# Norms of a latent attention placed between its projections, and products of split fp32 operands joined in pairs

## The reference

```python
# layer 0's mixer: sliding-window heads beside latent (MLA) heads
qa, ka, va, cq, ckv, kr = jnp.split(h @ w_in, EVEN_SPLITS, axis=-1)
qb = (rms_norm(cq, q_norm) @ w_uq)         # 384 -> 8 heads x (64 + 32 rotary)
kvb = (rms_norm(ckv, kv_norm) @ w_ukv)     # 256 -> 8 heads x (64 key + 64 value)
q_rope, k_rope = rope(q_rope, positions), rope(kr[:, :, None, :], positions)   # kr is shared by the heads
o = concat([window_attention(rope(qa), rope(ka), va), latent_attention(...)]) @ w_out
# gated network of the first block
x = x + (silu(h @ w_gate) * (h @ w_up)) @ w_down            # 1024 -> 2816 -> 1024
# second block: merge of three branches, then the last network
h = h + g1 * ((gp * (pool_o @ w_po) + gs * (sgu_o @ w_so) + ga * (attn_o @ w_ao)) @ w_o)
h = h + g2 * (square(relu(modulate(rms_norm_2(h)) @ w1)) @ w2)   # 1024 -> 4096 -> 1024
```

## Time and profile before

| | |
|---|---|
| median of 3 runs | 2077.81 us |
| profiled execution | 2079.3 us, its span 2077.5 us, mean granted clock 0.981 |
| busy | TensorE 97%, its weight loads 86%, VectorE 55%, ScalarE 43%, GpSimd 8% |
| matmuls | 14,920 |
| HBM read | 306.54 MB, 152 GB/s over the span |
| chain that ended last | TensorE 89%, VectorE 5%, ScalarE 2%, DMA 2% |

### The profile page before, as it was taken

The page is one execution under the profiler, slowest core; times in us unless marked ns, Lnnn a source line. Parts: engine busy times, 40 slices in busy tenths (PEclk is TensorE's granted clock), DMA queues, the critical chain, the costliest instruction groups (busy, mean ns, idle before and its releaser), DMA issues.

```text
span 2077.5 us, 35508 instructions
## 1 busy us (share of the span) xinstructions
PE 2007.5 (97%) x14920; PEld 1790.2 (86%) x14920; DVE 1139.2 (55%) x1987; ACT 888.3 (43%) x1498; POOL 165.5 (8%) x187
## 2 busy tenths in 40 slices
PE   7799999999999999999999999999999999999998
PEld 6759899999789999878688877777777987999998
DVE  6565565667556656524434445444444645666665
ACT  5464543444655445424532334322222435455443
POOL 0030000001203100002510000000000003000000
PEclk9899999999999999989999999999999999999999
DMA  7264589965647575313533324455454431664554
GB/s 222 66 194 155 152 221 218 228 183 161 226 143 190 177 216 170 107 41 121 160 101 98 107 84 142 157 162 174 158 166 143 127 92 30 184 196 146 183 183 132
DMA packets 331613, 317.71 MB, mean 153 GB/s; under 512 B 17061, under 2 KB 315820, under 8 KB 331198
## 3 DMA queue, kind: packets, MB, share of 16 engines
q1 hardware_dynamic: 326580, 301.64, 47.7%
q0 software_dynamic: 3904, 12.03, 3.0%
q10 hardware_dynamic: 970, 1.76, 0.3%
HBM read 306.54 MB, written 8.85 MB: 152 GB/s over the span
## 4 chain that ended last, share of the span: by engine, by line
PE 89%; DVE 5%; ACT 2%; DMA 2%; issue 1%; POOL 0%; ACTq 0%; DVEq 0%; POOLq 0%
PE acc L673 25%; PE acc L674 24%; PE acc L675 24%; DVE w_low L1894 2%; PE pss L838 2%; PE acc L688 1%; PE acc L689 1%; PE acc L690 1%; PE pst L850 1%; PE acc L761 1%; DMA raw<-in_l_w_up 1%; PE acc L821 1%; PE acc L865 1%; PE pso L865 1%; PE acc L789 1%
## 5 line engine op out<-in xcount | busy, mean ns | idle before, releaser
L1894 DVE TENSOR_TENSOR w_low<-raw,w_high 128x1024 fp32r<-128x1024 f32 (+4 forms) x503 | 560.5, 1154 | 174.5 <-ACT w_high L1371 173.7
L1371 ACT ACTIVATE w_high<-raw 128x1024 fp32r<-128x1024 f32 (+4 forms) x503 | 471.5, 984 | 398.7 <-PE acc L675 359.9
L673 PE MATMUL acc<-normed,w_high 128*128 128x256 f32 (+2 forms) x2008 | 636.7, 317 | 3.5 <-DVE w_low L1894 3.3
L674 PE MATMUL acc<-normed,w_high 128*128 128x256 f32 (+2 forms) x2008 | 631.3, 314 | 0.0
L675 PE MATMUL acc<-normed,w_low 128*128 128x256 f32 (+2 forms) x2008 | 630.9, 314 | 0.0
L673 PEld LDWEIGHTS acc<-normed,w_high 128*128 128x128 f32 (+1 forms) x2008 | 384.9, 192 | 32.4 <-DVE w_low L1894 4.4
L675 PEld LDWEIGHTS acc<-normed,w_low 128*128 128x128 f32 (+1 forms) x2008 | 385.0, 192 | 22.7
L674 PEld LDWEIGHTS acc<-normed,w_high 128*128 128x128 f32 (+1 forms) x2008 | 385.2, 192 | 22.1
L673 PE MATMUL acc<-inner,w_high 128*128 128x256 f32 (+2 forms) x1264 | 394.6, 312 | 3.4 <-DVE inner L1907 2.4
L674 PE MATMUL acc<-inner,w_high 128*128 128x256 f32 (+2 forms) x1264 | 391.8, 310 | 0.0
L675 PE MATMUL acc<-inner,w_low 128*128 128x256 f32 (+2 forms) x1264 | 391.2, 310 | 0.0
(11 more groups left out here) (255 smaller groups left out, 2123.2 us busy)
## 6 DMA issues: line engine op xcount, KB each, us to landing
raw<-in_w_ff SPq DMA_DIRECT2D x128, 512.0 KB, 4.4
raw<-in_w_mod SPq DMA_DIRECT2D x96, 512.0 KB, 4.6
raw<-in_w_in SPq DMA_DIRECT2D x84, 512.0 KB, 4.1
raw<-in_l_w_gate SPq DMA_DIRECT2D x44, 512.0 KB, 5.7
raw<-in_l_w_up SPq DMA_DIRECT2D x44, 512.0 KB, 4.7
raw<-in_l_w_down SPq DMA_DIRECT2D x32, 512.0 KB, 4.6
raw<-in_l_w_qkv SPq DMA_DIRECT2D x24, 512.0 KB, 4.4
raw<-in_l_w_out SPq DMA_DIRECT2D x16, 512.0 KB, 4.5
```

The lines of the kernel that those rows point to most:

```text
L673: mm(dst, lh, rh, start=i == 0, stop=False)
L674: mm(dst, lh, rl, start=False, stop=False)
L1371: nc.scalar.activation(WH[:, s % NSPLIT, w0:w0 + nw], RAW[:, r:r + nw], ACT.Copy)\
L1894: V.tensor_tensor(WL[:, s % NSPLIT, c], RAW[:, r:r + nw], WH[:, s % NSPLIT, c].bitcast(F32), ALU.subtract).then_inc(w_low, 1)
```

## The change

1. The query's mean square follows cq directly; its spread lies between the two tiles of ckv's unit; the rotations follow; the key's mean square lies between the query heads 0 to 3 and 4 to 5, its spread before the last two heads. ScalarE squares the query and takes its root before Silu and the sines, and the key after ckv's copy; VectorE makes both last sets of angles earlier, and norms the query before the rotations and the key after them. The sines have a semaphore of their own (`sin_done`), for which GpSimd and VectorE wait.
2. The shared rotary key leaves the lead: its sine product (`key_turned`) and its addition into eight heads (`key_spread`) stand in turns 1 and 2 of attention, behind the maxima.
3. `side_by_side` takes the place of `project` for output products and for the last network in layer 1, where there are 256 tokens: w_high meets high and low in one matmul of 512 columns that fills a bank, w_low x high goes onto its first half. Each bank then holds one tile in two halves, which the reader adds: `residual_sums` for the residual, and in the last network's input units a copy on ScalarE, two additions and a joined relu-square on VectorE. Excepted are the first unit of each mixer's output, layer 1's middle output stage of the gated network, and all products over 512 tokens.

The core of the diff (other places only follow the new count of banks):

```diff
 kr = wk(1792, 1, S, p0=64, p1=96)
+kr_turned = wk(3328, 1, S, p0=64, p1=96)
 cq = wk(2048, 3, S)
 ckv = wk(2816, 2, S)
-sq_cq, sq_ckv = wk(3328, 3, S), wk(4096, 2, S)
+sq_cq, sq_ckv = wk(3328, 3, S), view(BIAS, 2048, (2, S))
 mv = wk(2048, NB, 512)
...
+    def both(high, low):
+        return bass.AP(tensor=high.tensor, offset=high.offset,
+                       ap=[list(high.ap[0]), [low.offset - high.offset, 2], [1, S]])
+    def side_by_side(n, src, kt=KD, ready=None):
+        for i in range(n):
+            wh, wl = grid(take(kt, 2 * P), kt, 2 * P)
+            tiles = ([bank(), bank()],) if ready is not None and i == 0 else ([None], [None])
+            for n_group, group in enumerate(tiles):
+                if group[0] is None:
+                    group[0] = bank()
+                for k in range(kt):
+                    if ready is not None and i == 0:
+                        need(ready(k))
+                    high = src.high[:, k, 0:S]
+                    two = both(high, src.low[:, k, 0:S])
+                    for j, b in enumerate(group):
+                        m = j + n_group
+                        c = slice(P * m, P * m + P)
+                        out = b[:].rearrange("p (a n) -> p a n", a=2)
+                        if k == 0:
+                            mm(out, wh[:, k, c], two, start=True, stop=False)
+                            mm(b[:, 0:S], wl[:, k, c], high, start=False, stop=False)
+                        else:
+                            mm(b[:, 0:S], wl[:, k, c], high, start=False, stop=False)
+                            ins = mm(out, wh[:, k, c], two, start=False, stop=k == kt - 1)
+                            if k == kt - 1:
+                                ins.then_inc(acc_full, 1)
+            used()
...
             if u == 3:
-                pe.wait_ge(res_done, 1)
-                if k == KD - 1:
-                    copied(g)
+                copied(g + k - (KD - 1))
...
             project(1, at_pair, m=1)
-            project(1, at_pair)
             mean_square(sq_cq, 3, S)
+            w, b = grid(take(KD, 256), KD, 256), bank()
+            for m in range(2):
+                c = slice(P * m, P * m + P)
+                ins = product(b[:, S * m:S * m + S],
+                              [((w[0][:, k, c], w[1][:, k, c]),
+                                (at_pair.high[:, k, 0:S], at_pair.low[:, k, 0:S])) for k in range(KD)])
+                if m == 0:
+                    spread(S)
+            ins.then_inc(acc_full, 1)
+            used()
+            pe.wait_ge(const_in, 32)
+            rotate(swa_raw, const("rot64"), "swa", st["acc"] - 3)
+            st["store"] += 2
+            need(st["store"])
+            w = grid(take(3, 576), 3, 576)
+            turned(w, [96 * h for h in range(4)], cqn, 3, S, M=96)
...
             mean_square(sq_ckv, 2, S)
-            spread(S)
-            pe.wait_ge(const_in, 32)
-            rotate(swa_raw, const("rot64"), "swa", st["acc"] - 1)
+            turned(w, [96 * h for h in range(4, 6)], cqn, 3, S, M=96)
+            used()
             spread(S, at=S)
-            st["store"] += 3
-            need(st["store"])
-            turned(grid(take(3, 576), 3, 576), [96 * h for h in range(6)], cqn, 3, S, M=96)
-            used()
             turned(grid(take(3, 192), 3, 192), [0, 96], cqn, 3, S, M=96)
             used()
             heads = lambda x, k: x[:, k, :].rearrange("p (h d) -> p h d", h=8)[:, :, 64:128]
             def mla_lead():
                 wh, wl = w = grid(take(2, 1024), 2, 1024)
+                need(st["store"])
                 turned(w, [P * h for h in range(8)], ckvn, 2, S)
                 rotate(mla_raw, const("rot_mla"), "mla", st["acc"] - 5)
                 for t in range(NB):
                              for k in range(2)]).then_inc(acc_full, 1)
                 used()
-            attention(swa_tasks + mla_tasks, MODS, lead=mla_lead, tail=heads_product, late=SWA_H // 2)
+            st["store"] += 1
+            attention(swa_tasks + mla_tasks, MODS, lead=mla_lead, tail=heads_product, late=SWA_H // 2,
+                      keys=st["acc"] - 3)
...
         pe.wait_ge(cols_free, st["pair"])
-        project(3, ot)
...
         base = st["store"]
         st["store"] += KD
-        project(4, merged(T), T, ready=lambda k: base + k + 1)
+        if l:
+            side_by_side(4, merged(T), ready=lambda k: base + k + 1)
+        else:
...
             if kind == "in":
                 for m in range(tiles // 2):
-                    project(1, at_pair, T, ready=ready)
+                    if l:
+                        side_by_side(1, at_pair, ready=ready)
+                    else:
...
                 for m in range(D // cols):
-                    project(1, hidden(c, T), T, m=cols // P, kt=tiles)
+                    if l:
+                        side_by_side(1, hidden(c, T), kt=tiles)
...
                     if last and m:
-                        turn_out(m - 1, st["acc"] - 2)
...
+    pool.wait_ge(sin_done, 1)
...
-            copy_out(ckv, shape2)
-            split()
+            st["res"] = [st["acc"] - 2, st["acc"] - 1]
+            squares(cq, sq_cq, 3, S, res=True)
+            root(3, S)
             c = vcol["c_2"]
             nc.scalar.activation(SILC[:, :, 0:2].rearrange("p k s -> p s k"),
                                  VEC[:, c:c + 16].rearrange("p (s k) -> p s k", s=2), ACT.Silu)
             act.wait_ge(angles, 1)
-            nc.scalar.activation(ROPE[:], ROPE[:], ACT.Sin)
-            act.drain().then_inc(chain["act"], 1)
-            act.wait_ge(chain["act"], 1)
-            squares(cq, sq_cq, 3, S)
-            squares(ckv, sq_ckv, 2, S)
-            root(3, S)
+            nc.scalar.activation(ROPE[:], ROPE[:], ACT.Sin).then_inc(sin_done, 1)
+            split()
+            highs(chunks(cqn, 3, S))
+            copy_out(ckv, shape2)
+            st["res"] = [st["acc"] - 1]
+            squares(ckv, sq_ckv, 2, S, res=True)
+            split()
+            st["acc"] += 3
+            for i in range(2):
+                copy_out(mq[0:96, 2 * i:2 * i + 2, :], lambda b: shape2(b)[0:96], 96 ** -0.5)
             root(2, S, at=S)
-            st["acc"] += 3
-            highs(chunks(cqn, 3, S) + chunks(ckvn, 2, S))
-            for i in range(3):
-                copy_out(mq[0:96, 2 * i:2 * i + 2, :], lambda b: shape2(b)[0:96], 96 ** -0.5)
+            copy_out(mq[0:96, 4:6, :], lambda b: shape2(b)[0:96], 96 ** -0.5)
+            highs(chunks(ckvn, 2, S))
             split()
             copy_out(mq[0:96, 6:8, :], lambda b: shape2(b)[0:96], 96 ** -0.5)
             split()
...
-                    for n in banks(2, T):
+                    if l:
+                        for j in range(2):
+                            b, free = bank()
+                            nc.scalar.activation(SM[:, st["sig"] % 2, S * j:S * j + S], b[:, S:2 * S],
+                                                 ACT.Copy).then_inc(relu_done, 1)
+                        st["sig"] += 1
+                        highs([hidden(c, T).tiles(m, m + 2)])
+                    for n in banks(2, T) if l == 0 else ():
                         b, free = bank()
                         g, i = st["acc"] - 1, st["sig"]
...
+    def key_turned():
+        b, free = bank()
+        V.tensor_tensor(kr_turned[:, 0, :], b[64:96, 0:S], sin_mla(kr)[:, 0, :], ALU.mult).then_inc(free, 1)
+        st["rot"] += 1
+        own(free)
+    def key_spread():
+        rep = lambda a: bass.AP(tensor=a.tensor, offset=a.offset, ap=[list(a.ap[0]), [0, MLA_H], [1, S]])
+        dve.wait_ge(rot_done, st["rot"])
+        turned(V.tensor_tensor(mk[64:96, :, :], rep(kr), rep(kr_turned[:, 0, :]), ALU.add))
+    def rope(raw, sinv):
         dve.wait_ge(stored, st["store"])
         for i, r in enumerate(raw):
             b, free = bank()
...
-                rep = lambda a: bass.AP(tensor=a.tensor, offset=a.offset,
-                                        ap=[list(a.ap[0]), [0, MLA_H], [1, S]])
-                turned(V.tensor_tensor(wide, rep(r), rep(tmp), ALU.add))
-            else:
-                turned(V.tensor_tensor(r, r, tmp, ALU.add))
+            turned(V.tensor_tensor(r, r, tmp, ALU.add))
...
+        for k in m:
+            b, free = bank()
+            x = XC[:, k, 0:S]
+            for j in range(2):
+                half = b[:, S * j:S * j + S]
+                if gate is None:
+                    ins = V.tensor_tensor(x, x, half, ALU.add)
+                else:
+                    ins = V.scalar_tensor_tensor(x, half, MODC[:, gate + k, 0:1], x, ALU.mult, ALU.add)
+                if j == 0:
+                    link(ins)
+            ins.then_inc(free, 1)
+            own(free)
...
                 inverse(2 * j - 1)
+            if j <= len(between):
+                between[j - 1]()
...
             split()
             memory(0, 0, 2)
+            angle(2)
+            angle(3)
             split()
```

(46 more changed lines are left out.)

81 lines of the change are left out of this document (53 added, 28 removed).

## The result

The changed kernel takes 2057.8 us by the median (2054.95 to 2059.37, 4 runs) beside 2078.73 for the kernel before (2075.93 to 2083.92, 4 runs): a ratio of 0.9896 (95% interval 0.988 to 0.9913). The forecast was 2054.5 in a range of 2046 to 2063. The profiled execution took 2054.95, its span 2053.2, the lowest of the four; its granted clock is 0.989 where before had 0.981.

The account below looks back on a forecast made before the run. TensorE, busy 97% of the span, was taken as the bound, its longest gaps in layer 0's latent stage. Part 1's 14.7 us and part 2's 8.8 make 23.5, giving 2054.5 us, range 2046 to 2063.

Parts of the forecast that it names:

- part 1: Layer 0's latent stage: reordered norms and the rotary key's move remove waits and low clock, 14.7 us won.
- part 2: Output products and last network: 960 joined matmul triples save 11.9 us, less some losses, 8.8 us won.
- Compressed-key unit and query's norm: Latent stage: the query's squares fill a 2.46 us wait, its root lies under 24 matmuls; unit 5.8 us plus 1.5 low clock.
- The rotary key: Attention: its sine product and spreading leave the second maxima's 4.41 us wait, 2.9 us won, 0.7 left on the path.
- Size of joining: Products over 256 columns: 0.3476 us per triple instead of 0.360, 12.4 ns less, 11.9 us for 960.
- Input units of the last network: Last network: a longer chain to the low weights adds 0.3 us wait at every second of 16 units, 2.6 us lost.
- Layer 0's output stages: Layer 0's gated network: first two output stages can't outrun DMA transfers; 128 triples lose half of 1.6 us, 0.8.
- Output units at no cost: VectorE's four dependent operations, about 1 us more in 5.56, are hidden; uncovered, 44 units x 1 us.
- (a): Rival, joined products: joining saves nothing, as a joined start may cost two old ones; 2062.8 us, chance 0.08.
- (b): Rival, latent stage: VectorE's work becomes what it waits for, 7 us lost; 2061.5 us, chance 0.12.
- (c): Rival, joined products: the weight load shows, a triple takes 0.42 us, 58 us slower; 2120 us, chance 0.03.
- (d): Rival: nothing measurable; latent stage ends by another chain as long, joining worth 2 to 4 us; about 2075, chance 0.03.

Follow-up runs that it names:

- A: Stretch of the kernel, not a run: the latent mixer, from the mixers' entry to the product behind the mixer's output; 153.64 us before, 136.33 after.
- the run of that part alone: Latent stage's new order and the key's move on the kernel before, no joined matmul: 2064.05 us, ratio 0.9917.
- with half of it: Changed kernel with 8 of the 16 writes of the table of relative positions left out: 2059.66 us, ratio 0.9917; kernel before likewise: 2076.87 us, 0.9997.
- B: Stretch of the kernel, not a run: layer 0's gated network, up to the next mixer's first scores; 310.07 us before, 307.60 after.
- joining alone: Joined matmuls on the kernel before, with the latent stage's old order and the key in the lead: 2077.7 us, ratio 0.9982.
- C: Stretch of the kernel, not a run: layer 1, from the next mixer's first scores to the merge's entry; 337.94 us before, 336.72 after.
- D: Stretch of the kernel, not a run: the second block, from the merge's entry to the last network's first product; 1031.52 us before, 1030.56 after.
- E: Stretch of the kernel, not a run: the last network, from its first product to its last squares; 189.52 us before, 188.12 after.

## Why the forecast was right in sum, and which steps were off

The sum of 23.5 us came out at 20.9 and 22.3 by the medians (24.4 by the profiled executions), because an underestimate in part 1 (14.7 for some 17.4) and an overestimate in part 2 (8.8 for some 4) cancelled. The mechanisms are mostly as forecast; that the sum came so near is luck.

- **Compressed-key unit and query's norm.** Right in kind: the squares and the root lie under that unit, the spread inside it, and the query heads start behind the rotations. The unit starts 0.6 us sooner (0.2 forecast). The 1.5 us for a low clock after the wait did not come: the wait is 1.08, the 2.46 being filled by the mean square, and the clock stays at 1.00 in the window above. This term and the next 1.5 us for the clock made part 1 too small. The clock's share of A's gain is large, some 9 us by its windows; but for these 3 us the forecast has it, in the rates of its steps. The sine's place was tested by itself: 4.7 to 5.2 us.
- **The new wait before the key/value unit.** 2.2 forecast, 1.97 measured; the unit at 87.78 for "near 90". From the unit of the compressed key to it: 22.5 us for 23.4.
- **The low clock coming back there**, 1.5: it did so in 3 of the 9 profiles that share this order (16.1 us from the unit's start to the second maxima in six, 17.5 to 17.6 in three). As a certain term it was wrong; as a chance of one in three, which is an estimate from nine profiles, it is 0.5 us.
- **The rotary key.** 2.9 off the maxima's wait: 4.41 to 1.50, right to 0.1. What returns was put at 0.7 us; with the key put back, A grew by only 0.4 to 0.9, so 2.0 to 2.5 return, and by the spread of A it may be all. What the step missed is what stood behind that wait: before, the clock was down there (0.66 in 120 to 130 us) and other engines had time; after, at 1.00, TensorE meets a wait of 1.19 for GpSimd at 107.83 and one of 1.37 for modulation weights at 112.97.
- **Part 1** in all: 17.3 and 17.8 in A, less some 0.5 of its 48 joined pairs, or 17.4 by the run of that part alone; 14.7 forecast. From A's first product to the key/value unit's it is 15.3 us where 14.0 was forecast, and behind it 2.0 where 2.9 - 0.7 - 1.5 = 0.7 was.
- **Size of joining.** A pair of starts takes 0.349 us (output unit of 16 pairs, 5.59), where 0.3476 was forecast, so 10.6 ns saved per triple and not 12.4: 960 x 1.8 ns = 1.7 us too much. The 512-column start was taken from a row without a 256-column one between. With the 512 columns split the unit is back at 5.76, which is the same 10.6 ns.
- **Input units of the last network.** Right mechanism, too small: 2.6 us forecast, 3.55 found when the chain was shortened. The chain was forecast well (5.67 us measured); what was missing, as far as the rows show, is that the first start of 512 columns after a wait takes 0.34 us to the next instead of 0.23, and puts the next copy back with it.
- **Layer 0's output stages**, 0.8 lost to transfers: not borne out. TensorE's busy time there is 1.5 to 1.8 us less, near the full 1.9 of 176 pairs, with the whole table and with half of it. By B's length single pairs of profiles say 1.1 to 2.5, and joining alone has 0.9 more than before, because the waits and the clock differ from profile to profile.
- **Output units at no cost.** Failed at one place. In layer 1's network the residual's additions of a unit stand straight ahead of a split whose low weights TensorE wants next, and four of 1.78 us have taken the place of one of 0.68. VectorE before, and after:

```profile
822.22 0.68 DVE L2108 TENSOR_TENSOR resid<-resid,acc 128x512 f32<-128x512 f32 x1
822.94 1.83 DVE L1894 TENSOR_TENSOR w_low<-raw,w_high 128x768 fp32r<-128x768 f32 x2
```

```profile
799.36 1.78 DVE L2215 TENSOR_TENSOR resid<-resid,acc 128x256 f32<-128x256 f32 x4
801.17 1.83 DVE L1959 TENSOR_TENSOR w_low<-raw,w_high 128x768 fp32r<-128x768 f32 x2
```

  That is the wait of 1.46 at 803.05, in every joined profile (1.23 where the 512 are split). The cause was argued from the order of VectorE's list, and not tried by moving the split. It is about as large as what joining saves in starts in that layer (some 1.5 us): C shows no gain once the clock's drop is taken out.
- **Merge's output**: 1.1 forecast, 1.0 measured in D. From the start behind a wait of 1.00 us, 887 us into D, to the one behind a wait of 1.09, 1028 us into it, which holds the 64 joined pairs, it is 141.26 us before, 140.47 in both profiles of the changed kernel and 141.15 with the 512 split: 0.8 us, and the starts are nearly all of it.
- **Part 2** in all: 6.1 by the stretches B to E, 6.6 with A's pairs, 3.8 (1.5 to 6.2) by the run of joining alone; 8.8 forecast. The 6.6 holds C's 1.2, which are the clock's; without it, and with B's busy time for its length, it is 0.5 + 1.5 to 1.8 + 0 + 0.8 + 1.4 = 4.2 to 4.5 us, near the run. The terms that failed are the size of a start (1.7 us too much), layer 1's output units at no cost (some 1.5) and the last network's input units (1 too small).
- **Rivals.** (a) is out by the split of the 512 columns. (b) is out: VectorE's list holds the stretch up only for the 1.97 us forecast. (c) is out: a pair takes 0.349 us. (d) is out by the interval of the ratio, 2054 to 2061 us for its 2075.

## What to carry to other kernels

A norm's chain (squares, table, root, spread) costs next to nothing if it is cut into pieces that each lie under a product already waiting in line; look for what else its engine has been told to do first, a table and a sine in this case. What it costs is more than the waits: here half of A's gain was the clock that had fallen behind them. A wait that is taken away can come back behind, as the rotary key's did, so look at the stretch and not at the wait. When one operation is replaced by several small ones on an engine that also prepares the next weights, follow that engine's list at every stage and not at the steady one only: where the weights come next, put their split first. And judge a part by a stretch that repeats (here 0.1 us), since the whole moved by 2 to 5 us with the same program; where it does not repeat, read busy time, idle time and clock apart.

## What the runs showed of the chip that was not expected

- The drops of TensorE's granted clock belong in part to the execution and not to the program. In the 16 us behind the same wait of 1.97 it stayed at 1.00 in six profiles and fell in three, for 1.5 us each; what runs up to there is the same in all nine. The largest was at 50 to 60 us in one version: 0.53 with TensorE busy for 10.00 of 10 us, at a place where thirteen other profiles show none. That version's four executions have mean clocks of 0.984 to 0.986, the changed kernel's eight 0.986 to 0.989, though the programs are the same up to 290 us; why, is open. The Trainium skill says that what watches TensorE's activity runs freely and does not start with the kernel ("TensorE: Matmul & The Clock Gate", "What's actually happening"); the drops that come and go behind one wait fit that, and no run here tests it. By itself it does not account for the 10 us at 0.53 with TensorE busy throughout.
- Two starts of 256 columns in the place of one of 512 cost 10.6 ns more by a unit's length. A start behind a wait takes 0.1 us longer to the next: 0.34 us instead of 0.23 for 512 columns (changed kernel, at 803.05), 0.22 instead of 0.12 for 256 (kernel before, at 309.30 and 356.49).
- With the DMA rings 94% busy TensorE is busy for all of the 120 us from 280 to 400 in the changed kernel, and in its two profiles the stage is within 0.6 us of what it is with them 71% busy: a high share was no bound in these executions.
